# Splitting the second input product and laying the four attention heads between its units

## What is computed

```
proj = h @ w_in                      # 2048 x 6144
gb, gc, xc, q, k, v = split(proj)    # 1024 columns each
yc = gb * causal_dwconv(gc * xc, conv_w)               # 3 taps
# 4 heads, each with two maps (q, k of 128) and v of 256
s = q @ k.T * 128**-0.5 - slope * distance             # causal
attn = softmax(s of map 0) - lam * softmax(s of map 1)
yd = rms_norm(attn @ v, norm_g) * (1.0 - lambda_init)
y = concat([yc, yd]) @ w_out
x = layer_norm(ALPHA * x + (1.0 + g1) * y)
```

## Time and profile before

| | |
|---|---|
| median of 3 executions | 3176.61 us (3174.55 to 3177.65) |
| span of the profiled execution | 3174.3 us |
| TensorE matmul busy | 2725.0 us (86%) |
| VectorE busy | 2102.0 us (66%) |
| ScalarE busy | 1114.7 us (35%) |
| GpSimd busy | 474.7 us (15%) |
| DMA | 615.23 MB, mean 194 GB/s |
| chain that ended last | TensorE 68%, issue 14%, VectorE 10% |

### The profile page before, as it was taken

One profiled execution on the slowest core, in us unless ns is written; L12 is line 12 of the kernel. 1 busy time (PEld: TensorE's weight loads), 2 busy tenths in 40 slices (PEclk: granted clock), 3 DMA queues, 4 the chain that ended last, 5 costly groups with the idle time before them and its releaser, 6 DMA issues.

```text
span 3174.3 us, 52992 instructions
## 1 busy us (share of the span) xinstructions
PE 2725.0 (86%) x20804; PEld 2634.0 (83%) x20804; DVE 2102.0 (66%) x2410; ACT 1114.7 (35%) x1080; POOL 474.7 (15%) x614
## 2 busy tenths in 40 slices
PE   2388888466689799999999979994888999999997
PEld 1387777455579799999999979993888999999997
DVE  6879997666656677776767666674566754445444
ACT  0134444322213443333333343333334433333333
POOL 1059994111110000000000000000000000000000
PEclk6599999655669899999999989995889999999998
DMA  9753333222257477887787748771446765555551
GB/s 342 250 183 106 106 104 109 80 87 98 100 191 252 145 260 272 277 270 272 270 282 257 244 144 273 265 251 66 157 161 226 257 217 188 185 175 196 186 185 67
DMA packets 287556, 615.23 MB, mean 194 GB/s; under 512 B 22219, under 2 KB 22754, under 8 KB 286946
## 3 DMA queue, kind: packets, MB, share of 16 engines
q1 hardware_dynamic: 252642, 479.64, 44.6%
q0 software_dynamic: 34816, 134.23, 12.1%
HBM read 611.73 MB, written 2.10 MB: 193 GB/s over the span
## 4 chain that ended last, share of the span: by engine, by line
PE 68%; issue 14%; DVE 10%; POOL 4%; ACT 3%; DVEq 0%; DMA 0%; SPq 0%; POOLq 0%; ACTq 0%
PE groups L1448 21%; PE groups L1450 21%; PE groups L1452 21%; DVE w_lo L1104 2%; PE pm L1427 1%; PE pb L1481 1%; PE pa L1476 1%; ACT xT L982 1%; ACT act_hi L957 1%; POOL dn_mb L612 1%; DVE ada_acc L1287 1%; DVE s_z L1336 1%; DVE s_z L1343 1%; ACT w_hi L908 1%; DVE ada_acc L1094 1%
## 5 line engine op out<-in xcount | busy, mean ns | idle before, releaser
L1448 PE MATMUL groups<-act_hi,w_hi 128*128 128x256 f32 x4800 | 1379.7, 287 | 88.7 <-DVE w_lo L1104 47.0
L1450 PE MATMUL groups<-act_lo,w_hi 128*128 128x256 f32 x4800 | 1368.4, 285 | 0.0
L1104 DVE TENSOR_TENSOR w_lo<-w_raw,w_hi 128x2048 fp32r<-128x2048 f32 x388 | 895.1, 2307 | 713.8 <-ACT w_hi L908 712.2
L1452 PE MATMUL groups<-act_hi,w_lo 128*128 128x256 f32 x4800 | 1367.6, 285 | 0.0
L908 ACT ACTIVATE w_hi<-w_raw 128x2048 fp32r<-128x2048 f32 x386 | 738.4, 1914 | 1234.2 <-PE groups L1452 1233.8
L1448 PEld LDWEIGHTS groups<-act_hi,w_hi 128*128 128x128 f32 x4800 | 931.6, 194 | 104.8 <-DVE w_lo L1104 56.9
L1450 PEld LDWEIGHTS groups<-act_lo,w_hi 128*128 128x128 f32 x4800 | 932.0, 194 | 0.2
L1452 PEld LDWEIGHTS groups<-act_hi,w_lo 128*128 128x128 f32 x4800 | 931.2, 194 | 0.0
L1094 DVE SCALAR_TENSOR_TENSOR ada_acc<-ada_units,c_act,ada_acc 128x512 f32<-128x512 f32 x600 | 467.5, 779 | 19.3 <-DMA ada_units<-in_ada_w_dram 2.2
L1448 PE MATMUL groups<-hid_hi,w_hi 128*128 128x256 f32 x1408 | 390.9, 278 | 0.0
L1450 PE MATMUL groups<-hid_lo,w_hi 128*128 128x256 f32 x1408 | 390.2, 277 | 0.0
(11 more groups left out here) (324 smaller groups left out, 2221.8 us busy)
## 6 DMA issues: line engine op xcount, KB each, us to landing
ada_units<-in_ada_w_dram POOLq DMA_DIRECT2D x128, 1024.0 KB, 6.0
w_raw<-in_ffn_w_gate_dram SPq DMA_DIRECT2D x88, 1024.0 KB, 5.1
w_raw<-in_ffn_w_up_dram SPq DMA_DIRECT2D x88, 1024.0 KB, 5.2
w_raw<-in_ffn_w_down_dram SPq DMA_DIRECT2D x88, 1024.0 KB, 5.1
w_raw<-in_cd_w_in_dram SPq DMA_DIRECT2D x48, 1024.0 KB, 6.2
ada_units<-in_ada_w_dram SPq DMA_DIRECT2D x40, 1024.0 KB, 5.1
w_raw<-in_ab_w_in_dram SPq DMA_DIRECT2D x40, 1024.0 KB, 5.1
ada_first<-in_ada_w_dram SPq DMA_DIRECT2D x24, 1024.0 KB, 10.0
```

Source lines behind the costliest of these rows:

```text
L1104: dve.tensor_tensor(wlo[:, half], raw[:, slot], whi[:, half].bitcast(F32), ALU.subtract).then_inc(lo_done, 1)
L1448: pe.matmul(dst, whi[:, j % 2, kk, cols], hi[:, k], start=(k == 0 and n % 2 == 0), stop=False, skip_group_check=True)
L1450: pe.matmul(dst, whi[:, j % 2, kk, cols], lo[:, k], start=False, stop=False, skip_group_check=True)
L1452: last = pe.matmul(dst, wlo[:, j % 2, kk, cols], hi[:, k], start=False, stop=(k == UK * p["units"] - 1), skip_group_check=True)
```

## The change

`in1` becomes two products. `in1a` is q, k and v, three bodies of eight units with **two** `ada` blocks each, in a loop. `in1b` is the 24 units of gb, gc and xc as one straight body without `ada` units, in the order of groups gb, gc, xc for the first 512 columns and then for the second. The four heads are laid behind its units, six units a head: scores and v's transposes behind unit 0 of the six (`step == 0`), softmax weights (VectorE) at step 1, their transposes behind unit 2, the product with v behind unit 3, the norm at step 4. Of the short convolutions four stand at units 13, 15, 17 and 19 and four after the product. The attention uses the PSUM banks `pa`, `pb`, `pc` instead of `pg`. Scores are scaled on VectorE together with a bias that GpSimd prepares for each head (`dab`: four tensor_scalar of 128x384 in place of four memsets of a slope). Both key blocks of a head are handled in one step, with 13 steps on VectorE instead of 21. The result of a head goes into the place of its q in `pr1`. After the product `mixed_act` and `mixed_dve` split the four parts into `ahi` and `alo`, and `out1` takes its units in the order 2, 3, 0, 1, the attention's half first. The diff below leaves out most of the lines that are removed; they are in the functions printed above.

```
 
 
 
-ADA_AT = {(0, 4): [0] * 4, (0, 8): [0] * 8, (0, 12): [0] * 12, (1, 8): [0, 1, 1, 0, 0, 1, 1, 0],
+ADA_AT = {(0, 4): [0] * 4, (0, 24): [0] * 24, (0, 8): [0] * 8, (0, 12): [0] * 12, (1, 8): [0, 1, 1, 0, 0, 1, 1, 0],
           (1, 12): [0, 1, 0, 0, 1, 0, 0, 1, 0, 0, 1, 0], (2, 8): [1, 1, 1, 1, 1, 1, 2, 0]}
 ADA_SUM = {0: {}, 2: {4: 0, 7: 1}}
 ADA_TAKE = {0: {}, 2: {5: 0, 7: 1}}
@@ -92,13 +92,16 @@
     products[-1]["ada_after"] = 2 * HT // 2
...
-    add("in1", 6, [(w["in1"], GROUP * a, 2 * GROUP) for a, _ in pair], 4, ada=1)
+    add("in1a", 3, [(w["in1"], 3 * HALF + GROUP * a, 2 * GROUP) for a, _ in pair], 4, ada=2)
+    add("in1b", 1, [(w["in1"], HALF * part + GROUP * a, 0) for a, _ in pair for part in range(3)], 4)
     add("out1", 2, [(w["out1"], GROUP * a, 2 * GROUP) for a, _ in pair], 4, ada=1)
+    products[-1]["order"] = (2, 3, 0, 1)
     ffn(1, (1, 0, 0), 0)
...
+        def attention_act(act, i, j):
+            h, step = j // HEAD_UNITS, j % HEAD_UNITS
+
+            def done(ins):
+                ins.then_inc(daa.sem, 1)
+
+            def on(steps, name):
+                act.wait_ge(steps.sem, steps.at(h, name))
+
+            if j == 0:
+                act.wait_ge(da_sete.sem, 1)
+                act.activation(dav[:, LAMS:LAMS + 2], pb[:, 0:2], ACT.Exp).then_inc(da_seta.sem, 1)
+            if step == 0:
+                on(dae_, "vt")
+                done(act.activation(davt[:].rearrange("p a l -> p (a l)"), pc[:], ACT.Copy))
+                on(dad, "ng")
+                for b, s in enumerate((das0, das1)):
+                    for mp in range(2):
+                        n = 2 * b + mp
+                        last = act.activation(s[:, mp], s[:, mp], ACT.Exp, bias=dav[:, MAXES + n:MAXES + n + 1],
+                                              accum_out=dav[:, SUMS + n:SUMS + n + 1])
+                done(last)
+            elif step == 2:
+                on(dae_, "ct")
+                done(act.activation(dact[:].rearrange("p k l -> p (k l)"), pc[:, 0:3 * P], ACT.Copy))
+            elif step == 3:
+                on(dae_, "pv")
+                done(act.activation(das1[:].rearrange("p a l -> p (a l)"), pa[:], ACT.Square))
+            elif step == 4:
+                on(dae_, "ss")
+                done(act.activation(dastd[:], pb[:, L:2 * L], ACT.Sqrt, scale=1.0 / (2 * P), bias=consts[:, 0:1]))
+
+        def mixed_act(act):
             act.wait_ge(tile_used, by_name["out1"]["u0"])
+            for n, src in enumerate((pr1[:, Q:Q + 4], pr1[:, Q + 4:Q + 8], pr1[:, 0:4], pr1[:, 4:8])):
+                if n < 2:
+                    act.wait_ge(dad.sem, dad.at(2 * n + 1, "n"))
+                else:
+                    act.wait_ge(scd.sem, scd.at(4 * (n - 2) + 3, "g"))
+                k = UK * by_name["out1"]["order"][n]
+                act.activation(ahi[:, k:k + 4], src, ACT.Copy).then_inc(mix_hi, 1)
...
+        def attention_set_dve(dve):
+            dve.tensor_scalar(dav[:, GAIN:GAIN + 2], misc[:, 49:51], 1.0 - LAMBDA_INIT, None,
+                              ALU.mult).then_inc(da_setd.sem, 1)
             dve.tensor_tensor(dav[:, LAMS:LAMS + 2], misc[:, MQ:MQ + 3:2], misc[:, MQ + 1:MQ + 4:2],
                               ALU.mult).then_inc(da_setd.sem, 1)
+
+        def attention_dve(dve, i, j):
+            h, step = j // HEAD_UNITS, j % HEAD_UNITS
+
+            def done(ins):
+                ins.then_inc(dad.sem, 1)
+
+            def on(steps, name):
+                dve.wait_ge(steps.sem, steps.at(h, name))
+
+            if step == 0:
+                if j == 0:
+                    dve.wait_ge(da_setp.sem, 1)
+                on(dae_, "sc0")
+                done(dve.scalar_tensor_tensor(das0[:], pb[:, 0:L].rearrange("p (m l) -> p m l", m=2), P ** -0.5,
+                                              over(dab[:, h, 0:P], 2), ALU.mult, ALU.add))
+                on(dae_, "sc1")
+                done(dve.scalar_tensor_tensor(das1[:], pa[:].rearrange("p (m l) -> p m l", m=2), P ** -0.5,
+                                              over(dab[:, h, P:3 * P], 2), ALU.mult, ALU.add))
+                on(dad, "s0")
+                done(dve.tensor_reduce(dav[:, MAXES:MAXES + 2], das0[:], AX_X, ALU.max))
+                on(dad, "s1")
+                done(dve.tensor_reduce(dav[:, MAXES + 2:MAXES + 4], das1[:], AX_X, ALU.max))
+                on(dad, "mx1")
+                done(dve.tensor_scalar(dav[:, MAXES:MAXES + 4], dav[:, MAXES:MAXES + 4], -1.0, None, ALU.mult))
+                if j == 0:
+                    dve.wait_ge(da_seta.sem, 1)
+                    dve.scalar_tensor_tensor(dav[:, NEGLAM:NEGLAM + 1], dav[:, LAMS + 1:LAMS + 2], -LAMBDA_INIT,
+                                             dav[:, LAMS:LAMS + 1], ALU.add, ALU.subtract).then_inc(da_setd.sem, 1)
+            elif step == 1:
+                on(daa, "e")
+                done(dve.reciprocal(dav[:, SUMS:SUMS + 4], dav[:, SUMS:SUMS + 4]))
+                on(dad, "r")
+                if h == 0:
+                    dve.wait_ge(da_setd.sem, da_setd.at(0, "lam"))
+                done(dve.tensor_scalar(dav[:, SUMS + 1:SUMS + 4:2], dav[:, SUMS + 1:SUMS + 4:2],
+                                       dav[:, NEGLAM:NEGLAM + 1], None, ALU.mult))
+                on(dad, "rl")
+                for b, s in enumerate((das0, das1)):
+                    done(dve.tensor_scalar(dac[:, P * b:P * b + P * (b + 1)], s[:, 1],
+                                           dav[:, SUMS + 2 * b + 1:SUMS + 2 * b + 2], None, ALU.mult))
+                for b, s in enumerate((das0, das1)):
+                    on(dad, f"t{b}")
+                    part = dac[:, P * b:P * b + P * (b + 1)]
+                    done(dve.scalar_tensor_tensor(part, s[:, 0], dav[:, SUMS + 2 * b:SUMS + 2 * b + 1], part,
                                                   ALU.mult, ALU.add))
+            elif step == 4:
                 on(daa, "std")
+                done(dve.reciprocal(dastd[:], dastd[:]))
                 on(dad, "rr")
+                if h == 0:
+                    dve.wait_ge(da_setd.sem, da_setd.at(0, "gain"))
                 for f in range(2):
+                    last = dve.scalar_tensor_tensor(pr1[:, Q + 2 * h + f], pa[:, L * f:L * f + L],
+                                                    dav[:, GAIN + f:GAIN + f + 1], dastd[:], ALU.mult, ALU.mult)
                 done(last)
+            if j in (13, 15, 17, 19):
+                if j == 13:
+                    dve.wait_ge(grp_done, by_name["in1b"]["g0"] + 3 + 2)
+                short_conv(dve, (j - 13) // 2)
+
+        def mixed_dve(dve):
+            def low(n, src):
+                k = UK * by_name["out1"]["order"][n]
+                dve.wait_ge(mix_hi, n + 1)
+                dve.tensor_tensor(alo[:, k:k + 4], src, ahi[:, k:k + 4].bitcast(F32), ALU.subtract).then_inc(mix_lo, 1)
+            low(0, pr1[:, Q:Q + 4])
+            low(1, pr1[:, Q + 4:Q + 8])
+            low(2, pr1[:, 0:4])
+            dve.wait_ge(grp_done, by_name["in1b"]["g0"] + 6 + 2)
+            for t in range(4, 8):
+                short_conv(dve, t)
+            low(3, pr1[:, 4:8])
...
+        def attention_pe(pe, i, j):
+            h, step = j // HEAD_UNITS, j % HEAD_UNITS
+
+            def done(ins):
+                ins.then_inc(dae_.sem, 1)
+
+            def on(steps, name):
+                pe.wait_ge(steps.sem, steps.at(h, name))
+
+            if step == 0:
+                if h == 0:
+                    pe.wait_ge(da_seta.sem, 1)
+                else:
+                    pe.wait_ge(dad.sem, dad.at(h - 1, "n"))
+                for b, bank in enumerate((pb, pa)):
                     w = P * (b + 1)
                     for mp in range(2):
+                        last = pe.matmul(bank[:, w * mp:w * mp + w], pr1[:, Q + 2 * h + mp, P * b:P * b + P],
+                                         pr1[:, K + 2 * h + mp, 0:w], start=True, stop=True)
                     done(last)
                 for chunk in range(2):
                     for f in range(2):
+                        last = pe.transpose(q4(pc, 2 * chunk + f), pr1[:, V + 2 * h + f, P * chunk:P * chunk + P],
+                                            ident[:])
                 done(last)
+            elif step == 2:
+                on(dad, "c1")
+                on(daa, "vt")
+                for n in range(3):
+                    last = pe.transpose(q4(pc, n), dac[:, P * n:P * n + P], ident[:])
+                done(last)
+            elif step == 3:
+                on(daa, "ct")
                 for b in range(2):
                     for f in range(2):
                         for n in range(b + 1):
                             last = pe.matmul(pa[:, L * f + P * b:L * f + P * b + P], davt[:, n, P * f:P * f + P],
                                              dact[:, b + n], start=(n == 0), stop=(n == b))
+                done(last)
+            elif step == 4:
                 on(daa, "sq")
```

(27 more changed lines are left out.)

185 lines of the change are left out of this document (36 added, 149 removed).

## The result

The changed kernel took 3128.78 us (median of 4, 3126.05 to 3133.2) beside 3177.03 (median of 4) for the kernel before: ratio 0.9852, interval 0.9838 to 0.9865. The prediction was 3130, range 3114 to 3150. A second series of the same kernel later gave 3129.29 us, ratio 0.9851. The profiled execution has a span of 3124.4 us, 49.9 less than before, and it is one of the quicker ones; a second profile has 3129.4.

A forecast was written before the change was run, and what follows sets the result against it. TensorE was taken as the pace outside the attention, where it mostly waits in a chain of small steps. In `in1` +38.3, then -84.4 to `out1`'s fourth unit, gave -46.1: span 3128.2, plus 2.3, 3130 us; range 3114 to 3150.

The forecast's parts named there:

- E: End of `in1`'s last unit: 38.3 us later; from there to the end of `out1`'s fourth unit 36.1 instead of 120.5.
- The signs named: If right: `in1b` about 167 us, two stops near 5 at `out1`'s start, first `w_lo` near 1878, `ada_units` wait per body.
- Term 1: TensorE's new attention matmuls and transposes within the product: 4.5 us a head, +17.8 us, bounds 16 and 36.
- term 5: TensorE's stops inside `in1b`, at `c1` in heads 1 to 3 and at lambda in head 0: +10.4 us, bounds 5 and 18.
- Term 2: Start of `in1a`: four GpSimd scalings delay the `ada` loads and first `w_lo`: +6.4 us, bounds 2 and 8.5.
- Term 3: `in1a`, two `ada` blocks in eight units: 2.0 us a body, +4.0; old stops gone in `in1b`, -3.3.
- Term 4: Between `in1a` and `in1b`, TensorE waits for evacuated groups: 2.1 us, plus one more sum of 0.9: +3.0 us.
- Term 6: From the end of `in1`'s last unit to `out1`'s fourth unit's end: 36.1 replaces 120.5 us, -84.4.
- Loads as the bound: Rival in `in1a`: at 320 GB/s a body takes 52.4 us, 9.5 us more in all, 3140 us; chance 0.12.
- about 3 us higher: `in1a`'s loads at the skill's 341 GB/s: a body would take 49.2 us, making the sum about 3 us higher.
- Slow steps: Rival in `in1b`: semaphore trips make each of 16 attention steps stop TensorE 1.3 us longer: 3151 us; chance 0.08.
- lasting half clock: Rival: waits in `in1b` bring TensorE's clock to 1.2 GHz and it stays there: 3286 us; chance 0.05.

The follow-up runs named there:

- noattn: Changed kernel with the four attention heads left out of `in1b` on TensorE, ScalarE and VectorE, q going into `out1` unchanged: 3099.81 us, ratio 0.9765.
- even_ada: Changed kernel with `in1a`'s six `ada` blocks spread as three in `in1a` and three in `in1b`, four convolutions moved: 3115.26 us, ratio 0.9812.
- plain_order: Changed kernel with `out1`'s units back in order 0, 1, 2, 3, the mixes keeping their sequence: 3135.15 us, ratio 0.9871.
- seam: Changed kernel with the last gate group computed last in `in1b`, late convolution taps at positions 20 to 23, first mix copy and `low` before the last split: 3126.76 us.
- ones: Changed kernel with `in1a`'s eight `ada` units of a body one to a position, instead of two at position 6 and none at 7: 3128.06 us, ratio 0.985.

## Why the prediction was right, and where it was not

**What carries it.** The frame, two dates, held: E 38.3 later predicted, 40.3 and 44.9 measured; E to the fourth unit -84.4 predicted, -86.5 and -85.1 measured. The net is -46.2 in the first profile and -40.2 in the second, against -46.1. The rest up to the spans' differences (49.9 and 44.9) lies outside: ahead of the first split 2.2 and 1.0 us, behind the fourth unit 1.5 and 3.7, in code that is the same. So the median's difference of 48 us is met partly by luck: a term was too small and runs elsewhere were a little quicker. What these few microseconds outside are stays open; over all kernels here the first split begins between 1864.9 and 1870.7. The signs named came: the 24 units of `in1b` took 169.7 and 170.7 us instead of 167, there were two stops at the start of `out1` (5.7 and 2.8), the first `w_lo` of `in1a` began at 1876.03 in a profile that starts `in1` 2.2 us earlier than before, so at 1878.2 by the prediction's dates, and VectorE waited for `ada_units` in every body.

**Terms 1 and 5** (17.8 + 10.4 = 28.2): 26 to 27, by `noattn`. Term 1 is right: a head, from 2073.69 to 2113.53, takes 39.8 us where six units alone take 34.6; without the stop of 0.8 these are 4.5 us, as summed. Inside term 5 two errors cancel in part. The stops at `c1` are 0.8 and not 1.8: the score adds, for one, take 0.42 and 0.68 instead of the earlier trace rows's 0.48 and 0.75. The half clock behind the lambda stop cost more than the 1.0 I took: removing stop and clock together gave 4.9 to 5.9 although `da_c` took 0.6 more, so the clock was 2 to 3. The stop itself was 3.5 as summed, and its table load has the 1.28 of the earlier trace rows, the exponential right behind it:

```profile
2029.86 1.28 ACT L636 ACT_TABLE_LOAD   x1
2031.15 0.17 ACT L636 ACTIVATE da_vec<-pb 128x2 f32<-128x2 f32 x1
```

The Trainium skill's further drain of 1.38 us ("ScalarE: Activation LUTs", What ACT_TABLE_LOAD costs) isn't seen here either.

**Term 2** (+6.4): 6.5, and each step in it within 0.3 us once the 2.2 us are taken off by which this profile starts `in1` earlier. The scaling was the one price without a row; 1.2 was right (1.22).

**Term 3** (+4.0, then -3.3): the step that failed. The removed stops are right: before, from unit 23 to E, there are 3.3 us above 24 units and three sums. The added ones were put at 2.0 us in two bodies and the third as hidden; from unit 2 to unit 23 the changed kernel has 131.0 and 134.5 us where 21 units and five sums are 125.4, so 5.6 and 9.1. The late second load is there, and the stop of 2.0 was near: it measured 1.9 and 1.4 us in the first profile, 2.4 and 3.1 in the second. What was put at nothing without a reason is the half clock behind it, 0.4 and 1.8, then 1.9 and 1.7 us; I charged it only behind the long stops. I also named the wait at `w_lo` alone, and part of the stop stands at the `ada` sum. So spreading the units evenly over a body, as the mechanism suggests, left a stop of 1.6 us at the sum. A price for "two blocks in eight units" had to be taken from VectorE's whole cycle: 5.40 of 5.76 us leaves no room for the position at which the sum needs its unit early.

**Term 4** (+3.0): unit 24 takes 10.2 and 12.2 us against 6.65 for a unit and a sum, 3.6 and 5.6 more where 2.1 was predicted. TensorE's stops there are 1.6 us in the first profile (0.6 at the sum, 1.0 at the copy) and 2.1 in the second, and most of the rest is again half clock, 0.51 from 2020 to 2023 in the first. The doubled position is not needed for it: `even_ada`, without one, takes 10.5.

**Term 6** (36.1): 34.0 and 35.5. The first stop was 5.7 instead of 5.0. The second was 2.8 instead of 4.8: 0.7 of the difference is the longer first stop, which moved TensorE, and 1.3 are the four convolutions, each 2.3 instead of 2.7. Their operations have the same lengths, but stand 0.04 us apart where they stood 0.15 apart before; the new code gives them fixed addresses in place of computed ones, and whether that is the cause was not tested. This stop comes from where it was put: the fourth copy is queued ahead of the split at 2205.33. `plain_order` (2.9 to 4.4 us more) and `seam` (7.3 to 8.8 less) show both ends of that queue.

**The rivals.** Loads as the bound: the demand was met. The Trainium skill's 341 GB/s for loads of 1 MB ("DMA: Bandwidth & Descriptors", Bandwidth) is near what `in1a` drew, 336 in this window of the changed kernel, and yet `ones` shows no load waited for beyond 0.7 us:

```profile
1880.00:1970.00 90.00, 86.65 (x703) 86.08 (x702) 74.72 (x76) 30.45 (x18) 11.24 (x15) 0.97 0.94 336
```

The prediction's "about 3 us higher" by that figure doesn't follow from its own sums: three bodies of 49.2 us are 147.6, where 147.7 were summed. Slow steps and a lasting half clock did not occur; after 2050 the clock in `in1b` is 1.00.

## What to carry to other kernels

A chain of small steps that stands alone costs its length (77 us for four heads), and between the units of a product that doesn't need it, it costs less than twice its matmuls (26 to 27 us, of which 18 are the matmuls); cut it so that every step has a unit of slack, and look at what runs free under a wait today, as the table load did, before moving a step. Background work that fills an engine's cycle (5.40 of 5.76 us) must be spread over a longer stretch: at this density an even spread within a body (`ones`) still left a stop at each sum, and half of it moved to `in1b` (`even_ada`) left none in `in1a`. When a gain of a few microseconds can't be told in the medians, dates of unit ends in the two traces tell it in place, provided that one knows from several profiles how much the stretches around it vary.
